# In the second half of a leg's rows, the up-rows are fetched up to twenty ahead of the down-rows

## The chip, the cores and the metric

The kernel runs on one core of one Trainium2 chip. The metric is the device time of one execution in microseconds. PE is TensorE, DVE is VectorE, ACT is ScalarE, POOL is GpSimd, SP is SyncE.

## The reference

Two layers of a hybrid encoder over 512 positions of 1024 features. Each layer adds a mix of three head groups to x, and then a retrieval from a table of 16384 experts (PEER). The part that sets this kernel's time is the retrieval, cut to its core:

```python
s1, s2 = scores of a query against 128 sub-keys each
v1, i1 = lax.top_k(s1, 16); v2, i2 = lax.top_k(s2, 16)
cand = v1[..., :, None] + v2[..., None, :]
top_s, pos = lax.top_k(cand, 16)            # per head, 8 heads
experts = take_along_axis(i1*128 + i2, pos) # 8 x 16 = 128 experts per position
gates = softmax(top_s)
act = gelu(einsum('tkd,td->tk', peer_u[e], h))
out = einsum('tk,tkd->td', gates * act, peer_v[e])
```

So each position needs 128 rows of `peer_u` and 128 rows of `peer_v`, each 1024 float32.

## The kernel before

The 512 positions are 4 tiles of 128, one position in each partition, and there are two layers, so 8 tiles pass. The program runs in ten legs, n = 0 to 9, one behind the other, with a meeting of all engines between two. Leg n computes the mixers and the routing (the choice of experts) of tile n, and beside them the retrieval of tile n-1. "First" tiles of a layer (legs 0 and 4) have more to do and tables of their own. Leg 8 has no mixers left, and leg 9 ends the last tile. Below, "leg 2" is n = 2. Leg 1 starts at 251.83 us of the span.

**Up-rows** are fetches of `peer_u`: k-th expert of all 128 positions, 128 rows of 4 KB, into one of 8 buffers `ringU` (`fetch_u`, L226). VectorE multiplies each with h and sums it: a **dot** (`gathered`, L803; semaphore `dots`). A leg takes 128 of them; the first eight go by `idx_w` at the end of the leg before, the others by `idx_g`. The first fetch by `idx_w` is used here as the mark of a leg's start. **Down-rows** are fetches of `peer_v` into 8 buffers `ringV` (`fetch_v`, L236). TensorE mixes them in groups of four rows with the weights `wm` (`mix`, L479; semaphore `mixed`); a group is 16 matmuls in the trace and 8 with two column halves in the order's rows. A leg fetches 128 down-rows: 56 for the second half of tile n-2's experts (its first eight were fetched at the end of the leg before), then 64 for the first half of tile n-1's, then eight ahead for the next leg. Leg 1 has no tile n-2 and leaves out the 56. Numbered 1 to 128 in GpSimd's order, down-row j belongs to ring row j+7.

All fetches are issued by GpSimd, in one queue and in program order. Its loop goes in steps of four rows, r0 = 8, 12, ... 124: four up-rows, then four down-rows. It waits before each: up-row k (from 1) for `dots` of k-8 at least, down-row j for `mixed` of j at least. Only the first comes before the second in the queue, so a wait for a dot also holds back the down-rows behind it, and the other way round.

The engines' other work is laid between by tables of counts: `DOTS` says how many dots VectorE has done by each stage (`heads`, `values`, `x1`, `queries`, `routing`), `MIX` how many groups TensorE has mixed by then. `queries` is the point just ahead of the routing. The routing on VectorE starts with sixteen MAX8 over the key scores (L1207, waits for TensorE's L733), then FIND_INDEX8 and MATCH_REPLACE8 (L1210, L1211), MAX8 and FIND_INDEX8 again (L1216, L1219), the candidates (L1226 to L1239), their second eight (L1243, L1246), the gates (L1253) and the expert numbers (L1286 to L1299). It has seven gaps in which dots are done, the seven numbers of `routing`: behind eight and sixteen fields, behind L1219, behind L1239, behind L1246, and two in the expert numbers.

Weights of 2 MB a piece come by SP's queue: w_in, w_out and peer_w_q, into two buffers `wring`.

## Time and profile before

| | us |
|---|---|
| median of 3 runs | 3650.46 (3648.02 to 3655.35) |
| the profiled execution | 3636.02 |
| its span, first to last instruction | 3634.2 |
| VectorE busy | 2227.8 (61%) |
| GpSimd busy | 2283.0 (63%) |
| TensorE busy | 1836.1 (51%) |
| DMA, mean over the span | 353 GB/s |

Durations are read from one profiled execution and set against its own time. In the timelines below a row starts with its start and its duration in us; the bracket at its end has the idle time of the engine just before it and what ended that. "issue" there means that the profile shows nothing that was waited for.

### The profile page before, as it was taken

Reading aid. Unit: us, or ns where it says so; the run is one execution under the profiler, and the core shown is the slowest. Engines: PE = TensorE matmul, PEld = TensorE weight load, DVE = VectorE, ACT = ScalarE, POOL = GpSimd, SP = SyncE. Lnnn points to the kernel's source line nnn. Section 1 sums busy time; section 2 is a strip of 40 time slices with the busy share of each in tenths; the row PEclk is TensorE's granted clock in tenths of the full one; section 3 lists DMA queues with packets and bytes.
Section 4 is the critical chain, followed back from the end, with each engine's and each line's share of the span. In section 5 each row is a group of like instructions: output and inputs, shape, how many; then the busy total and the mean of one; then the engine's idle time right before and its main releaser. Section 6 shows DMA issues by size and latency. Waiting matters only on the chain.

```text
span 3634.2 us, 30323 instructions
## 1 busy us (share of the span) xinstructions
PE 1836.1 (51%) x10176; PEld 894.3 (25%) x10176; DVE 2227.8 (61%) x5807; ACT 250.6 (7%) x683; POOL 2283.0 (63%) x2067
## 2 busy tenths in 40 slices
PE   6825452736454562566636455465636465233333
PEld 4425230513132230231304122232304122000000
DVE  6267757675768557765486746676585856645420
ACT  1200100001000100101000010001000110000000
POOL 0015667677667667555666766777676776767653
PEclk9767575767677776776758677676857676555666
DMA  6547899999999999999999999999999999999996
GB/s 247 211 158 267 302 409 342 357 369 390 379 352 368 337 406 364 407 415 405 382 375 374 349 360 396 343 378 361 398 370 366 358 370 412 361 362 378 361 344 232
DMA packets 314671, 1282.62 MB, mean 353 GB/s; under 512 B 34955, under 2 KB 35211, under 8 KB 303507
## 3 DMA queue, kind: packets, MB, share of 16 engines
q0 software_dynamic: 294912, 1073.87, 78.2%
q1 hardware_dynamic: 18740, 201.83, 13.7%
q10 hardware_dynamic: 864, 4.99, 0.4%
q8 instruction: 82, 1.34, 0.1%
q14 instruction: 73, 0.59, 0.0%
HBM read 1272.16 MB, written 8.39 MB: 352 GB/s over the span
## 4 chain that ended last, share of the span: by engine, by line
POOL 31%; PE 18%; DVE 16%; DMA 16%; issue 14%; another core or an unknown queue 5%; ACT 1%; SPq 0%; POOLq 0%; DVEq 0%; ACTq 0%
POOL ringV L236 18%; POOL ringU L226 13%; DMA ringV<-in_peer_v,idxP 9%; PE py L479 6%; DVE ringU L803 5%; DMA ringU<-in_peer_u,idx_g 5%; PE pj L551 4%; DMA ringU<-in_peer_u,idx_w 2%; PE pj L718 1%; PE pj L622 1%; PE pj L494 1%; PE pj L558 1%; PE pw L692 1%; PE pw L519 1%
## 5 line engine op out<-in xcount | busy, mean ns | idle before, releaser
L803 DVE CUSTOM_DVE_ANT_0 ringU<-ringU,h2g 128x1024 f32<-128x1024 f32 x1024 | 1224.6, 1225 | 800.0 <-DMA ringU<-in_peer_u,idx_g 549.7
L236 POOL DMA_INDIRECT ringV<-in_peer_v,idxP x1024 | 1144.6, 1118 | 581.4 <-issue 272.3
L479 PE MATMUL py<-ringV,wm 128*32 128x512 f32 x4096 | 817.8, 914 | 1125.2 <-DMA ringV<-in_peer_v,idxP 924.8
L226 POOL DMA_INDIRECT ringU<-in_peer_u,idx_g x960 | 1071.4, 1116 | 472.1 <-issue 284.2
L479 PEld LDWEIGHTS py<-ringV,wm 128*32 128x32 f32 x4096 | 160.3, 145 | 1646.9 <-issue 1575.9
L551 PE MATMUL pj<-hT,wring 128*128 128x128 f32 (+1 forms) x2560 | 329.8, 292 | 26.7 <-issue 18.8
L551 PEld LDWEIGHTS pj<-hT,wring 128*128 128x128 f32 (+1 forms) x2560 | 317.4, 201 | 63.3 <-issue 50.7
L226 POOL DMA_INDIRECT ringU<-in_peer_u,idx_w x64 | 62.2, 971 | 269.4 <-DVE gate_w L1299 246.1
L692 PE MATMUL pw<-hT,ckv_all 128*128 128x128 f32 x320 | 78.9, 401 | 94.1 <-issue 60.7
L718 PE MATMUL pj<-wring,mixT 128*128 128x512 f32 x256 | 118.3, 622 | 9.1 <-issue 8.4
L494 PE MATMUL pj<-ident,wk 128*128 128x128 f32 x168 | 43.5, 364 | 138.6 <-DVE wk L1165 61.3
L519 PE MATMUL pw<-wring,crep 128*32 128x512 f32 x384 | 67.1, 811 | 73.2 <-DVE crep L886 29.6
L829 DVE TENSOR_TENSOR py<-py,g2g 128x1024 f32<-128x1024 f32 x8 | 9.8, 1231 | 142.8 <-PE py L479 130.6
L494 PE MATMUL pj<-ident,hh 128*128 128x128 f32 x128 | 30.9, 422 | 119.4 <-DVE hh L1033 115.9
L678 PE MATMUL pw<-ckvT_all,hh 128*128 128x128 f32 (+3 forms) x128 | 65.7, 618 | 50.3 <-DVE cols L1171 40.1
L692 PEld LDWEIGHTS pw<-hT,ckv_all 128*128 128x128 f32 x320 | 61.8, 278 | 114.4 <-issue 67.6
L803 DVE DVE_READ_ACCUMULATOR2_ANT acts<- 128x1 f32 x1024 | 82.7, 81 | 0.0
L622 PE MATMUL pj<-wk,par 128*32 128x128 f32 x384 | 50.1, 356 | 49.1 <-DVE state L1084 38.6
L718 PEld LDWEIGHTS pj<-wring,mixT 128*128 128x128 f32 x256 | 50.6, 201 | 81.3 <-issue 80.2
L318 ACT ACTIVATE hT<-pj 128x512 f32<-128x512 f32 (+3 forms) x96 | 47.0, 489 | 336.5 <-PE pj L494 195.9
L494 PEld LDWEIGHTS pj<-ident,wk 128*128 128x128 f32 x168 | 25.3, 178 | 178.9 <-issue 97.0
L408 ACT ACTIVATE wk<-wk,cols 128x128 f32<-128x128 f32 (+3 forms) x64 | 35.8, 560 | 470.2 <-DVE cols L1171 291.9
(294 smaller groups left out, 1893.0 us busy)
## 6 DMA issues: line engine op xcount, KB each, us to landing
wring<-in_w_in SPq DMA_DIRECT2D x28, 2048.0 KB
wring<-in_w_mod SPq DMA_DIRECT2D x24, 2048.0 KB
wring<-in_w_out SPq DMA_DIRECT2D x16, 2048.0 KB
wring<-in_peer_w_q SPq DMA_DIRECT2D x16, 2048.0 KB
ringV<-in_peer_v,idxP POOLq DMA_INDIRECT x1024
ringU<-in_peer_u,idx_g POOLq DMA_INDIRECT x960
wring<-in_w_in SPq DMA_DIRECT2D x8, 784.0 KB
x_mix<-xs SPq DMA_DIRECT2D x8, 512.0 KB
```

The lines of the kernel that those rows point to most:

```text
L226: pool.indirect_dma_start(out=ringU[k % NR][:, :], out_offset=None, in_=ux, in_offset=bass.IndirectOffsetOnAxis(ap=idx[:, k:k + 1], axis=0 ...
L236: pool.indirect_dma_start(out=ringV[r % NR][:, :], out_offset=None, in_=vx, in_offset=bass.IndirectOffsetOnAxis(ap=idx[:, at:at + 1], axis=0),
L318: a.activation(dst, src, ACT.Copy).then_inc(S[sem], 1)
L479: mm = t.matmul(py[32 * j:32 * j + 32, c * 512:(c + 1) * 512], wm[e % 2][:, at:at + 32], ringV[(4 * m + j) % NR][:, c * 512:(c + 1) * 512] ...
L494: m = t.transpose(dst, src, ident[:, :])
L519: mm = t.matmul(pw[32 * j:32 * j + 32, at:at + 512], crep[:, k * 32:(k + 1) * 32], wt[:, k * 512:(k + 1) * 512], start=k < 4, stop=k >= 4)
L551: mm = t.matmul(dst, wt[:, k * gc + c0:k * gc + c0 + width], hT[:, k * 128:(k + 1) * 128], start=k == 0, stop=k == KT - 1)
L622: mm = t.matmul(dst, C[:, cs], wk[:, at + m * 128:at + (m + 1) * 128], start=i == 0, stop=i == 3)
L678: t.matmul(pw[:, (h % 2) * 512:(h % 2) * 512 + W], q, ckvT_all[:, 0:W], start=True, stop=True).then_inc(S["lg_ps"], 1)
L692: mm = t.matmul(pw[:, 1024 + (h % 4) * 128:1152 + (h % 4) * 128], ckv_all[:, s * 128:(s + 1) * 128], hT[:, (h % 2) * 512 + s * 128:(h % 2) ...
L718: mm = t.matmul(pj[n][:, :], mixT[:, k * 128:(k + 1) * 128], wt[:, k * 512:(k + 1) * 512], start=k == 0, stop=k == KT - 1)
L803: v.tensor_tensor_reduce(out=ringU[k % NR][:, :], in0=ringU[k % NR][:, :], in1=h2g[:, :], scale=1.0, scalar=0.0, op0=ALU.mult, op1=ALU.add ...
```

## The change

In the legs whose tile is not the first of a layer and that have mixers (1, 2, 3, 5, 6, 7), GpSimd's loop fetches, from r0 = 64 on, up-rows further than the step's own four: `ups_by` gives the number of groups of four that are fetched by step i = r0/4. It is i+1 as before below 16, and i+1+(i-15)//2 from there, 128 rows at most. So steps 17, 19, 21, 23 and 25 have eight up-rows, and 128 are reached in step 26. `DOTS` lets VectorE do more of them ahead of the routing (106 where there were 95), and `MIX` has one or two groups fewer by each stage from the last head on (21 where there were 23 ahead of the key scores; the semaphores' limits are unchanged). `MIX_FIRST` is written without `MIX` as its base and keeps its numbers.

```diff
@@ -58,15 +58,15 @@
-        "picked": [38 + (r + 1) * 10 // 16 for r in range(16)], "heads": [48 + (h + 1) * 26 // 8 for h in range(8)],
-        "values": 82, "x1": 83, "queries": 95, "routing": [101, 107, 113, 117, 120, 122, 124]}
+        "picked": [38 + (r + 1) * 10 // 16 for r in range(16)], "heads": [48 + (h + 1) * 28 // 8 for h in range(8)],
+        "values": 86, "x1": 89, "queries": 106, "routing": [110, 113, 116, 119, 121, 123, 125]}
...
-       "heads": [12, 13, 14, 15, 16, 16, 16, 18], "values": 19, "x1": 20, "h2": 21, "queries": [22, 23], "routing": 28}
+       "heads": [12, 13, 14, 15, 16, 16, 16, 17], "values": 18, "x1": 19, "h2": 20, "queries": [21, 21], "routing": 27}
@@ -80,6 +80,11 @@
+def ups_by(b, i):
+    n = i + 1 if b is None or is_first(b) or 4 * i < HE else i + 1 + (i - 15) // 2
+    return min(n, T // 4)
@@ -238,11 +243,13 @@
+                up = NR
                 for r0 in range(NR, T, 4):
                     if u is not None:
-                        for r in range(r0, r0 + 4):
+                        for r in range(up, 4 * ups_by(b, r0 // 4)):
                             pool.wait_ge(S["dots"], r - NR + 1)
                             fetch_u(r, idx_g)
+                        up = 4 * ups_by(b, r0 // 4)
```

GpSimd at the end of leg 2, from step 26 (before), to the first fetches for the next leg (x4 means four fetches):

```order
L226 DMA ringU<-in_peer_u,idx_g 128x1024 x4
L236 DMA ringV<-in_peer_v,idxP 128x1024 x4
L226 DMA ringU<-in_peer_u,idx_g 128x1024 x4
L236 DMA ringV<-in_peer_v,idxP 128x1024 x4
L226 DMA ringU<-in_peer_u,idx_g 128x1024 x4
L236 DMA ringV<-in_peer_v,idxP 128x1024 x12
L226 DMA ringU<-in_peer_u,idx_w 128x1024 x8
```

The same queue after, from step 23:

```order
L231 DMA ringU<-in_peer_u,idx_g 128x1024 x8
L241 DMA ringV<-in_peer_v,idxP 128x1024 x4
L231 DMA ringU<-in_peer_u,idx_g 128x1024 x4
L241 DMA ringV<-in_peer_v,idxP 128x1024 x4
L231 DMA ringU<-in_peer_u,idx_g 128x1024 x8
L241 DMA ringV<-in_peer_v,idxP 128x1024 x4
L231 DMA ringU<-in_peer_u,idx_g 128x1024 x4
L241 DMA ringV<-in_peer_v,idxP 128x1024 x32
L231 DMA ringU<-in_peer_u,idx_w 128x1024 x8
```

Down-rows 97 to 128 now stand behind the last up-row in one piece of 32, where the longest was 12. All line numbers behind the tables are higher by five to seven.

TensorE in leg 2 before, from the projection of the outputs (L718) to the end of the mixing; L733 are the key scores, L551 the queries:

```order
L718 MATMUL pj<-wring,mixT 128x512 x16
L479 MATMUL py<-ringV,wm 32x512 x8
L494 MATMUL pj<-ident,hh 128x128 x8
L479 MATMUL py<-ringV,wm 32x512 x8
L551 MATMUL pj<-hT,wring 128x128 x32
L479 MATMUL py<-ringV,wm 32x512 x8
L551 MATMUL pj<-hT,wring 128x128 x32
L479 MATMUL py<-ringV,wm 32x512 x8
L733 MATMUL pw<-par,pr 128x128 x16
L479 MATMUL py<-ringV,wm 32x512 x72
```

And after (L725, L558 and L740 are those three):

```order
L725 MATMUL pj<-wring,mixT 128x512 x16
L486 MATMUL py<-ringV,wm 32x512 x8
L501 MATMUL pj<-ident,hh 128x128 x8
L486 MATMUL py<-ringV,wm 32x512 x8
L558 MATMUL pj<-hT,wring 128x128 x32
L486 MATMUL py<-ringV,wm 32x512 x8
L558 MATMUL pj<-hT,wring 128x128 x32
L740 MATMUL pw<-par,pr 128x128 x16
L486 MATMUL py<-ringV,wm 32x512 x88
```

Two groups of down-rows moved behind the key scores: eleven groups stand there instead of nine.

## Rows read from the trace of the kernel before

**Rows 1.** The page, part 3: GpSimd's DMA queue, packets, MB, share of 16 engines.

```profile
q0 software_dynamic: 294912, 1073.87, 78.2%
```

**Rows 2.** Busy time by stretch, leg 2 (stretch, us, each engine's, PEclk, DMA share, GB/s).

```profile
869.30:937.00 67.70, 39.87 (x253) 26.39 (x251) 33.69 (x98) 4.45 (x10) 39.51 (x38) 0.74 1.02 411
969.30:1027.90 58.60, 19.44 (x92) 4.56 (x92) 47.91 (x142) 0.84 (x3) 45.11 (x37) 0.61 0.92 326
```

**Rows 3.** Timeline of POOL: the starts of legs 2, 3, 5, 6, 7, 8.

```profile
619.27 0.94 POOL L226 DMA_INDIRECT ringU<-in_peer_u,idx_w  x1 [0.30 <-issue]
1027.98 0.94 POOL L226 DMA_INDIRECT ringU<-in_peer_u,idx_w  x1 [0.30 <-issue]
1910.17 0.93 POOL L226 DMA_INDIRECT ringU<-in_peer_u,idx_w  x1 [4.39 <-DVE acts L803]
2321.67 0.94 POOL L226 DMA_INDIRECT ringU<-in_peer_u,idx_w  x1 [0.30 <-issue]
2731.02 0.93 POOL L226 DMA_INDIRECT ringU<-in_peer_u,idx_w  x1 [0.30 <-issue]
3139.77 0.94 POOL L226 DMA_INDIRECT ringU<-in_peer_u,idx_w  x1 [0.30 <-issue]
```

**Rows 4.** Timeline of DVE: the routing's first MAX8, legs 2, 5, 7.

```profile
925.22 0.89 DVE L1207 MAX8 pr<-pw 128x8 f32<-128x128 f32 x4 [6.80 <-PE pw L733]
2213.16 2.08 DVE L1207 MAX8 pr<-pw 128x8 f32<-128x128 f32 x10 [1.44 <-PE pw L733]
3036.12 2.08 DVE L1207 MAX8 pr<-pw 128x8 f32<-128x128 f32 x10 [2.12 <-PE pw L733]
```

**Rows 5.** Timeline of PE: second group behind the key scores, legs 2, 5, 7.

```profile
938.76 1.94 PE L479 MATMUL py<-ringV,wm 128*32 128x512 f32 x8 [8.42 <-DMA ringV<-in_peer_v,idxP]
2232.05 2.79 PE L479 MATMUL py<-ringV,wm 128*32 128x512 f32 x12 [6.58 <-DMA ringV<-in_peer_v,idxP]
3054.35 1.94 PE L479 MATMUL py<-ringV,wm 128*32 128x512 f32 x8 [6.58 <-DMA ringV<-in_peer_v,idxP]
```

**Rows 6.** Timeline of DVE: starts and ends of the routing's pieces, leg 2.

```profile
932.77 1.21 DVE L803 CUSTOM_DVE_ANT_0 ringU<-ringU,h2g 128x1024 f32<-128x1024 f32 x1
...
941.07 0.09 DVE L1210 MATCH_VALUE_LOAD pr<-pr,pw 128x8 f32 x1
...
945.32 1.22 DVE L803 CUSTOM_DVE_ANT_0 ringU<-ringU,h2g 128x1024 f32<-128x1024 f32 x1
...
953.82 3.19 DVE L1216 MAX8 pr<-wk 128x8 f32<-128x128 f32 x16
...
962.12 0.29 DVE L1219 FIND_INDEX8 pr<-pr,wk 128x8 uint32<-128x128 f32 x1 [1.07 <-issue]
...
973.99 0.68 DVE L1226 TENSOR_TENSOR wk<-pr 128x512 f32<-128x512 f32 x1
...
980.75 1.23 DVE L803 CUSTOM_DVE_ANT_0 ringU<-ringU,h2g 128x1024 f32<-128x1024 f32 x1
...
985.34 1.50 DVE L1243 MAX8 pr<-wk 128x8 f32<-128x112 f32 x8
...
988.96 1.22 DVE L803 CUSTOM_DVE_ANT_0 ringU<-ringU,h2g 128x1024 f32<-128x1024 f32 x1
...
990.11 1.22 DVE L803 CUSTOM_DVE_ANT_0 ringU<-ringU,h2g 128x1024 f32<-128x1024 f32 x1
```

**Rows 7.** Timeline of POOL: two waits among the last tile's down-rows.

```profile
3533.63 0.94 POOL L236 DMA_INDIRECT ringV<-in_peer_v,idxP  x1 [3.84 <-PE py L479]
...
3547.22 0.94 POOL L236 DMA_INDIRECT ringV<-in_peer_v,idxP  x1 [3.97 <-PE py L479]
```

**Rows 8.** Timeline of POOL: the fetch of down-row 65 in leg 3.

```profile
1260.35 0.93 POOL L236 DMA_INDIRECT ringV<-in_peer_v,idxP  x1 [6.57 <-PE py L479]
```

**Rows 9.** Busy time by stretch, leg 3, columns as in Rows 2.

```profile
1248.00:1268.00 20.00, 14.49 (x86) 8.05 (x84) 11.22 (x24) 4.28 (x11) 10.68 (x11) 0.69 0.69 236
```

**Rows 10.** Timeline of POOL: a fetch beside dots in the routing, leg 2.

```profile
970.59 1.99 POOL L236 DMA_INDIRECT ringV<-in_peer_v,idxP  x1 [0.30 <-issue]
```

More of the change, by code:

```diff
@@ L67 @@
 MIX = {"start": 1, "projected": [2, 3, 4, 5], "states": 6, "gated": 7, "picked": 11,
-       "heads": [12, 13, 14, 15, 16, 16, 16, 18], "values": 19, "x1": 20, "h2": 21, "queries": [22, 23], "routing": 28}
-MIX_FIRST = dict(MIX, mod=[0, 1, 1, 2, 9, 10, 11, 11, 12, 13, 14, 14], start=3, projected=[4, 6, 7, 8], states=10, gated=12,
+       "heads": [12, 13, 14, 15, 16, 16, 16, 17], "values": 18, "x1": 19, "h2": 20, "queries": [21, 21], "routing": 27}
+MIX_FIRST = dict(mod=[0, 1, 1, 2, 9, 10, 11, 11, 12, 13, 14, 14], start=3, projected=[4, 6, 7, 8], states=10, gated=12,
                  picked=15, heads=[15, 16, 16, 16, 18, 19, 19, 20], values=21, x1=22, h2=23, queries=[24, 25], routing=29)
```

## The prediction, made before the changed kernel was run

> **What bounds the kernel now.** I read the page's DMA queues first. GpSimd's queue moves 1073.87 MB and its packets fill 78.2% of 16 engines' span [rows 1]. The code makes 256 row fetches for each of 8 tiles, 2048 in all, so one fetch is 0.524 MB. The reader should see a kernel whose time is nearly that of its gathers. Everything else matters only where it delays one.
>
> Second, the table by stretch for leg 2 [rows 2]. From 869 to 937 us DMA moves 411 GB/s, one fetch per 0.524/0.411 = 1.28 us. In the last 59 us before the next leg only 326 GB/s move, while VectorE is busy 47.9 of 58.6 us. That is the routing stretch which the change thins out.
>
> Third, the marks of a leg. A leg starts with the first fetch by idx_w [rows 3]: leg 2 lasts 1027.98-619.27 = 408.7 us, leg 5 411.5, leg 7 408.8. Routing starts at the first MAX8 on the key scores [rows 4]: 305.9, 303.0 and 305.1 us into the leg. I call this point S. VectorE had waited there for TensorE's key scores (6.8, 1.4, 2.1 us), not for up-rows: its 95 dots were done. From S to the leg's end it takes 102.8, 108.5 and 103.7 us.
>
> So two things decide: when S comes, and how long the rest takes from S. The changed legs are 1, 2, 3, 5, 6 and 7. Legs 4 and 8 keep their order.
>
> **First part: S comes later.** I count the fetches of a leg in GpSimd's order, 1 to 256 (leg 1 lacks 56 down-rows, equally before and after). Before, dot 95 needs fetch 179: up-row 95 stands behind 84 down-rows. After, the table wants 106 dots before routing, and up-row 106 stands behind 84 down-rows: fetch 190. Running ahead does not hide this: the same bytes must land, in order, and from 869 to 937 us the queue has no hole in which eleven more could have come.
>
> When fetch 190 lands can be read. Down-rows 89 to 92 are fetches 189 to 192 before. TensorE mixes them as the second group behind the key scores and waits for exactly that landing [rows 5]: 938.76, 2232.05, 3054.35 us, or 319.5, 321.9, 323.3 us into legs 2, 5, 7. Fetch 190 is two earlier, 2.6 us; the dot on it takes about 1.2. So S would be 318.1, 320.5, 321.9: later by 12.2, 17.5 and 16.9 us. The other edits ahead of S (two dots more for the heads, four for values, six for x1) I cost at nothing. Their up-rows have the same fetch numbers as before or up to six more, and the wait for fetch 190 covers them; without that cover it would be six fetches, 7.7 us.
>
> **Second part: from S to the leg's end.** Moving 11 dots out takes 11 x 1.15 = 12.6 us of VectorE's time from routing. But GpSimd has one queue, and up-row k may be fetched only when dot k-8 is done. Down-row 97 now stands behind up-row 128, so behind dot 120. Dot 120 comes in the fifth gap of routing. With the durations of leg 2 [rows 6]: S to the first gap 932.77-925.22 = 7.55; then dots 107-110, 4.6 (a dot follows the last after 990.11-988.96 = 1.15); 945.32-941.07 = 4.25, three dots 3.45; 962.41-953.82 = 8.6 (end of the last FIND_INDEX8), three dots 3.45; 980.75-973.99 = 6.76, three dots 3.45; 988.96-985.34 = 3.62, dot 120, 1.15. Sum 46.9. Up-row 128 is then fetched, and down-row 97 starts at S+48.2.
>
> Behind it stand 32 down-row fetches in a row, where before the longest such run was 12. Only 8 buffers hold them, each free only when TensorE has mixed it. Leg 8's end shows such a run [rows 7]: GpSimd waits for TensorE at 3533.63 and again at 3547.22, eight fetches per 13.59 us. So down-row 121 starts three such rounds behind 97, 40.8 us, and its eight take 8 x 1.24 = 9.9, since a fetch that waits for nothing takes 0.94 and follows 0.30 behind the last [rows 3]. The leg ends at S+48.2+50.7 = S+98.9.
>
> That is shorter than now by 3.9, 9.6 and 4.8 us in legs 2, 5, 7. With the later S the legs become longer by 8.3, 7.9 and 12.1: mean 9.4, times six legs 56.6 us.
>
> **Third part: what the run-ahead fills.** In leg 3, GpSimd waits 6.57 us for TensorE before down-row 65, and DMA falls to 236 GB/s over 20 us [rows 8, 9], 3.5 MB or 8.5 us below the rate of 411. After, four more up-rows (77 to 80) are queued ahead of that wait; more can't be, since every later block of down-rows waits at the same fetch number. That returns at most 4 x 1.28 = 5.1 us a leg where the hole is deep, and nothing where there is none. Leg 3's hole is the only one shown, and I take 3 us as the mean of legs with deep and with shallow ones: 18 us for six. The bounds are 0 and 31.
>
> **The port.** Beside back-to-back dots a fetch takes 1.99 us of GpSimd instead of 0.94 [rows 10]. The cost of the dots that remain in routing lies between 0 (GpSimd waits there anyway) and two fetches per leg, 2.1 us. I take 0. The Trainium skill's page SBUF — State Buffer, section "SBUF: two separate sides", says that VectorE with two SBUF inputs and GpSimd share a port pair under an exclusive lock. The doubled fetch agrees with it. By that rule alone taking dots away from a stretch that GpSimd's issuing bounds would be a gain; it is the rival "faster" below. The skill's page DMA: Bandwidth & Descriptors, section "Anatomy of one DMA — SWDGE (gpsimd) path", gives 2.0 us plus bytes/436e3, which would be 3.2 us a fetch and would make the run of 32 faster than I have it; the 13.59 us round speaks against relying on it.
>
> **Sum.** 56.6-18 = +38.6 us on the profiled execution, 3636.0 us (span 3634.2 and 1.8 around it): 3674.6. The median of the runs shown, 3650.5, lies 14.4 above that execution, so 3689.
>
> **Rivals.** *Faster: routing is relieved and S stays.* If eleven more up-rows land by the time the key scores are there, each leg ends at the old S+98.9: -3.9, -9.6, -4.8, mean 6.1, six legs -37, so 3614. If filled holes come on top, less by up to 18: 3596. For it: VectorE is the busiest engine in the last 59 us, and DMA there has room (326 of 411 GB/s). Against: fetch 190 landed 11 to 16 us after S in the three legs [rows 4, 5]. It decides from a gain of about 9 to 13 fetches ahead of S, where at most 4 are in sight. Chance 0.22.
> *Nothing moves.* The holes give the whole 5.1 us, and the run of down-rows goes at 12 us a round, three rounds 4.8 us a leg, 29 for six: 56.6-31-29 is about zero, 3650. For it: groups of down-rows that follow a pause find TensorE idle. Chance 0.12. The change not doing what it says comes out here too: "up to twenty ahead" exists in the order alone, since the ring holds eight; were the landing order hardly altered, nothing would move.
> *Much slower: GpSimd's one queue waits twice.* If TensorE's groups behind the key scores also starve while up-rows 113 to 128 wait for dots, the ring is empty when the run of 32 begins, and one more round of 13.6 us a leg is lost: +38.6+82, 3771. Against: groups of down-rows 89 to 96 stand between. Chance 0.06.
>
> **How the numbers follow.** Forecast 0.60, with its own range from its bounds: holes at 5.1 us and no port cost, 56.6-31 = +26 (3676), to no holes and the port's 12.6, +69 (3720). The range of 0.8 must reach into the faster rival to leave no more than 2 in 10 out: 3614 to 3720. About 0.2%, 7 us, is what a measurement of this kernel can tell from no change. Faster 0.23, same 0.12, slower 0.65.
>
> **What would show it.** Right: MAX8 on the key scores starts 315 to 322 us into legs 2, 5, 7 after a wait for an up-row's DMA; GpSimd waits for dots before up-rows 115, 122, 125 and 128; the last 32 down-rows take rounds near 13.6 us with TensorE as releaser; the leg is 412 to 421 us; dot 128 is done well ahead of the leg's end. Wrong: S at 306 with no wait for DMA, which gives the faster rival; or rounds of 12 us and less; or DMA above 400 GB/s until the last down-rows. If up-row 106 has another fetch number than 190, the first part falls.

## The result, and the profile of the changed kernel

The changed kernel takes 3708.23 us (median of 4 runs, 3703.64 to 3710.77). The kernel before, run beside it, takes 3649.24 us (4 runs, 3643.87 to 3655.35). The ratio is 1.0155 with the interval [1.0127, 1.0183]: slower by 59 us, where the forecast was slower by 38.6. The profiled executions lie further apart, 3710.77 against 3636.02 us, or 74.8.

The page of the changed kernel: part 3, GpSimd's DMA queue, and of part 4 the chain by engine. The bytes are those of [rows 1] and spread over a longer span, so the share falls from 78.2% to 77.5%.

```profile
q0 software_dynamic: 294912, 1073.87, 77.5%
...
POOL 29%; DVE 21%; DMA 17%; PE 16%; issue 12%; another core or an unknown queue 4%; ACT 0%; SPq 0%; POOLq 0%; DVEq 0%; ACTq 0%
```

The marks of a leg come first, as in [rows 3]: the timeline of POOL with the first fetch by idx_w of legs 2, 3, 5, 6, 7 and 8 (start, duration, instruction, idle time before it and what ended it).

```profile
629.17 0.94 POOL L231 DMA_INDIRECT ringU<-in_peer_u,idx_w  x1 [0.30 <-issue]
...
1052.24 0.94 POOL L231 DMA_INDIRECT ringU<-in_peer_u,idx_w  x1 [0.30 <-issue]
...
1940.45 1.19 POOL L231 DMA_INDIRECT ringU<-in_peer_u,idx_w  x1 [0.30 <-issue]
...
2361.43 0.94 POOL L231 DMA_INDIRECT ringU<-in_peer_u,idx_w  x1 [0.30 <-issue]
...
2787.13 0.94 POOL L231 DMA_INDIRECT ringU<-in_peer_u,idx_w  x1 [0.30 <-issue]
...
3216.35 0.94 POOL L231 DMA_INDIRECT ringU<-in_peer_u,idx_w  x1 [0.30 <-issue]
```

S, the first MAX8 of routing, is read as in [rows 4], in the timeline of DVE, legs 2, 5 and 7:

```profile
950.93 2.27 DVE L1214 MAX8 pr<-pw 128x8 f32<-128x128 f32 x11 [4.99 <-PE pw L740]
...
2260.24 2.86 DVE L1214 MAX8 pr<-pw 128x8 f32<-128x128 f32 x14
...
3113.66 2.47 DVE L1214 MAX8 pr<-pw 128x8 f32<-128x128 f32 x12
```

Leg 2 lasts 1052.24-629.17 = 423.1 us, of which 950.93-629.17 = 321.8 lie ahead of S. All legs, both kernels, read in the same way:

| leg | length before | after | S before | after | S to the end, before | after |
|---|---|---|---|---|---|---|
| 1 | 367.4 | 375.8 | 260.7 | 274.9 | 106.7 | 100.9 |
| 2 | 408.7 | 423.1 | 305.9 | 321.8 | 102.8 | 101.3 |
| 3 | 413.4 | 423.6 | 311.5 | 322.1 | 101.9 | 101.5 |
| 5 | 411.5 | 421.0 | 303.0 | 319.8 | 108.5 | 101.2 |
| 6 | 409.3 | 425.7 | 303.7 | 325.6 | 105.6 | 100.1 |
| 7 | 408.8 | 429.2 | 305.1 | 326.5 | 103.7 | 102.7 |

Leg 4, whose order is unchanged, goes from 468.8 to 464.7 us. The six changed legs give +79.3 us: S comes later by 100.8 us in all, and what follows S is shorter by 21.5. With leg 4 that makes +75.2 us, and the profiled executions lie 74.8 apart. Counted by S, the loss lies ahead of S, and what follows pays back about a fifth of it. This split should not be read as the place of the loss: S marks another point of the queue in each kernel, fetch 179 before and fetch 190 after. Fetch by fetch it looks different, as the run of the kernel before again shows below.

What follows S is seen in leg 7. The timeline of POOL, from up-row 115 to down-row 121 (L231 fetches up-rows, L241 down-rows):

```profile
3122.71 1.68 POOL L231 DMA_INDIRECT ringU<-in_peer_u,idx_g  x1 [6.91 <-DVE acts L810]
...
3142.51 1.68 POOL L231 DMA_INDIRECT ringU<-in_peer_u,idx_g  x1 [3.16 <-DVE acts L810]
...
3159.83 1.68 POOL L231 DMA_INDIRECT ringU<-in_peer_u,idx_g  x1 [2.91 <-DVE acts L810]
3161.82 0.94 POOL L241 DMA_INDIRECT ringV<-in_peer_v,idxP  x1 [0.30 <-issue]
...
3176.16 1.75 POOL L241 DMA_INDIRECT ringV<-in_peer_v,idxP  x1 [2.43 <-PE py L486]
...
3190.68 0.94 POOL L241 DMA_INDIRECT ringV<-in_peer_v,idxP  x1 [2.21 <-PE py L486]
...
3203.13 0.94 POOL L241 DMA_INDIRECT ringV<-in_peer_v,idxP  x1 [0.84 <-PE py L486]
```

The first three rows are up-rows 115, 122 and 128, each waiting for a dot. Directly behind up-row 128 stands down-row 97, at 3161.82-3113.66 = S+48.2. The last three are down-rows 105, 113 and 121: rounds of 14.3, 14.5 and 12.5 us per eight, with TensorE's mixing as releaser, and 13.2 us more to the leg's end. Dots are no longer what ends a leg: in leg 7 dot 128 is done at 3182.5, 34 us ahead of the end. Before, down-row 97 was fetched 22 to 24 us behind S, and 79 to 85 us followed it.

Busy time by stretch (stretch, its us, busy time and instructions of PE, PEld, DVE, ACT and POOL, then PEclk, DMA share, GB/s), ahead of S in leg 2 and for the run of last down-rows in leg 7:

```profile
881.00:949.00 68.00, 33.90 (x209) 23.90 (x202) 32.36 (x60) 4.00 (x8) 40.13 (x39) 0.69 1.02 412
...
3165.00:3216.00 51.00, 20.12 (x108) 4.48 (x108) 19.30 (x41) 1.45 (x6) 32.38 (x30) 0.67 0.88 302
```

The first answers to the 411 GB/s of [rows 2]. The second is the new tail: VectorE is busy only 19.3 of 51 us, where before it was busy 47.9 of 58.6 ([rows 2], leg 2), yet DMA moves 302 GB/s instead of 326. VectorE was relieved there and the transfers became no faster.

### The profile page after: what moved, and what is told of

Its sections match the earlier page's. It is cut to its first block, busy times and chain, and to the rows that moved or that the text cites. A ratio compares the mean times of both kernels' runs of the same rounds, so it can differ in the third digit from the quotient of the medians.

```text
span 3709.0 us, 30323 instructions
## 1 busy us (share of the span) xinstructions
PE 1867.9 (50%) x10176; PEld 911.5 (25%) x10176; DVE 2224.7 (60%) x5807; ACT 252.2 (7%) x683; POOL 2298.9 (62%) x2067
## 3 DMA queue, kind: packets, MB, share of 16 engines
q0 software_dynamic: 294912, 1073.87, 77.5%
q10 hardware_dynamic: 864, 4.99, 0.3%
## 4 chain that ended last, share of the span: by engine, by line
POOL 29%; DVE 21%; DMA 17%; PE 16%; issue 12%; another core or an unknown queue 4%; ACT 0%; SPq 0%; POOLq 0%; DVEq 0%; ACTq 0%
POOL ringV L241 16%; POOL ringU L231 13%; DVE ringU L810 8%; DMA ringV<-in_peer_v,idxP 7%; DMA ringU<-in_peer_u,idx_g 7%; PE py L486 6%; PE pj L558 4%; DMA ringU<-in_peer_u,idx_w 2%; PE pj L629 1%; PE pj L725 1%; DVE pr L1217 1%; DVE wk L1218 1%; DVE pr L1226 1%; PE pj L501 1%
## 5 line engine op out<-in xcount | busy, mean ns | idle before, releaser
L241 POOL DMA_INDIRECT ringV<-in_peer_v,idxP x1024 | 1132.2, 1106 | 608.2 <-PE py L486 279.0
L231 POOL DMA_INDIRECT ringU<-in_peer_u,idx_g x960 | 1097.2, 1143 | 508.5 <-issue 278.1
L486 PE MATMUL py<-ringV,wm 128*32 128x512 f32 x4096 | 832.4, 916 | 1087.5 <-DMA ringV<-in_peer_v,idxP 860.7
L558 PE MATMUL pj<-hT,wring 128*128 128x128 f32 (+1 forms) x2560 | 328.5, 292 | 20.5 <-issue 11.5
L558 PEld LDWEIGHTS pj<-hT,wring 128*128 128x128 f32 (+1 forms) x2560 | 316.4, 202 | 56.1 <-issue 43.6
L231 POOL DMA_INDIRECT ringU<-in_peer_u,idx_w x64 | 64.7, 1010 | 266.9 <-DVE gate_w L1306 247.7
L725 PE MATMUL pj<-wring,mixT 128*128 128x512 f32 x256 | 117.4, 618 | 10.7 <-issue 8.5
L501 PEld LDWEIGHTS pj<-ident,hh 128*128 128x128 f32 x128 | 25.1, 223 | 189.2 <-DVE hh L1040 162.1
L725 PEld LDWEIGHTS pj<-wring,mixT 128*128 128x128 f32 x256 | 50.2, 199 | 78.7 <-issue 75.2
```

The source lines that it names most:

```text
L231: pool.indirect_dma_start(out=ringU[k % NR][:, :], out_offset=None, in_=ux, in_offset=bass.IndirectOffsetOnAxis(ap=idx[:, k:k + 1], axis=0 ...
L241: pool.indirect_dma_start(out=ringV[r % NR][:, :], out_offset=None, in_=vx, in_offset=bass.IndirectOffsetOnAxis(ap=idx[:, at:at + 1], axis=0),
L486: mm = t.matmul(py[32 * j:32 * j + 32, c * 512:(c + 1) * 512], wm[e % 2][:, at:at + 32], ringV[(4 * m + j) % NR][:, c * 512:(c + 1) * 512] ...
L501: m = t.transpose(dst, src, ident[:, :])
L558: mm = t.matmul(dst, wt[:, k * gc + c0:k * gc + c0 + width], hT[:, k * 128:(k + 1) * 128], start=k == 0, stop=k == KT - 1)
L725: mm = t.matmul(pj[n][:, :], mixT[:, k * 128:(k + 1) * 128], wt[:, k * 512:(k + 1) * 512], start=k == 0, stop=k == KT - 1)
```

## The experiments

Theory: GpSimd has one queue in order. Down-rows stand behind up-rows whose dots the routing does late, so a leg ends when up-row 128 is fetched, plus a run of 32 down-rows through 8 buffers; and S moves with up-row 106's place in the queue. Rivals: the late S alone is the loss; the dots for x1 hold up the mixers; TensorE's mixing sets the run's pace.

The kernel before took about 3570 us beside the kernels that follow, not 3649. So each kernel is set against the runs of before that were made beside it, by ratio; a difference in us between two kernels that were not run side by side is rough.

**The changed kernel again.** No edit: a base for the rest.

> The changed kernel itself, beside the others of this call, because the kernel before took 3570 us beside the last four runs where it had taken 3649: times of different calls can't be set against one another, their ratios can. First measurement: 1.0155. On the faster memory of the last call, S came at 318 to 320 us; theory (one queue) says S+48.2 for down-row 97 whatever the memory, and S+101 to 102 for the leg's end, so that the ratio is no lower there: 1.015 to 1.025.

3651.02 us, 1.0217 [1.02, 1.0234]. S stands at 315.3 to 321.9 us in legs 2, 3, 5, 6 and 7, and the leg ends at S+101 to S+102.8, with down-row 97 at S+48.1 or S+48.2 in every changed leg. More frequent here are GpSimd's waits for dots ahead of S. Its timeline in leg 7, 272.8, 275.4 and 308.0 us into the leg:

```profile
3036.51 0.94 POOL L231 DMA_INDIRECT ringU<-in_peer_u,idx_g  x1 [4.35 <-DVE acts L810]
3039.03 1.78 POOL L231 DMA_INDIRECT ringU<-in_peer_u,idx_g  x1 [1.58 <-DVE acts L810]
...
3071.70 1.81 POOL L231 DMA_INDIRECT ringU<-in_peer_u,idx_g  x1 [9.44 <-DVE acts L810]
```

These are up-rows 98, 99 and 109. Up-row 98 needs dot 90, and the stage x1 allows 89; dot 90 comes only behind the norm. Up-row 109 needs dot 101, and that dot waits for no stage but for its own row, in the timeline of DVE:

```profile
3070.20 1.22 DVE L810 CUSTOM_DVE_ANT_0 ringU<-ringU,h2g 128x1024 f32<-128x1024 f32 x1 [10.02 <-DMA ringU<-in_peer_u,idx_g]
```

Up-row 101 was fetched at 3047.52, 22.7 us earlier. So the longest of these waits is a wait for the transfers. In the first measurement's leg 3 the wait before up-row 98 is 4.98 us:

```profile
1333.24 1.68 POOL L231 DMA_INDIRECT ringU<-in_peer_u,idx_g  x1 [4.98 <-DVE acts L810]
```

**The kernel before again.**

> The kernel before, for a trace beside the last two calls' traces: ratio 1.000. With it e7's gain of 0.8% can be placed. Theory: in e7 no fetch of the last 54 waits for a dot of routing, so that from down-row 97 to the leg's end it takes 78.5 us (read in e7), 2 to 5 us less than in the kernel before, and the rest of the 5 us a leg comes from waits for dots ahead of down-row 97 that go away.

3558.02 us, where the runs of the same kernel beside it have 3570.53: 0.9973 [0.9949, 0.9996]. Two sets of runs of one kernel lie 0.3% apart, so a ratio within 0.3% of 1 proves nothing here. Against its legs, those of the changed kernel again have S later by 12.9 us on average and 0.6 us more behind S: 13.5 us a leg, six legs 81, near the 79 us between 3651.02 and the 3572.11 beside it. What follows S is no shorter here, so the 21.5 us that it gave back in the first measurement are not repeated.

The same fetch of GpSimd's queue can be set against itself. Its start, in us into the leg, mean of legs 2, 3, 5, 6 and 7 (read from the timelines of POOL):

| | fetch 190 | fetch 210 | fetch 250 | the leg's end |
|---|---|---|---|---|
| before | 303.2 | 336.6 | 399.1 | 410.3 |
| changed | 303.9 | 344.7 | 414.3 | 424.5 |
| before again | 301.2 | 335.3 | 394.3 | 406.1 |
| changed again | 296.9 | 339.1 | 409.4 | 420.0 |

Fetches 190 and 250 of leg 2, before again (the leg starts at 616.64) and then changed again (626.67):

```profile
920.87 0.94 POOL L236 DMA_INDIRECT ringV<-in_peer_v,idxP  x1 [0.30 <-issue]
...
1012.26 1.20 POOL L236 DMA_INDIRECT ringV<-in_peer_v,idxP  x1 [0.30 <-issue]
```

```profile
921.80 0.94 POOL L231 DMA_INDIRECT ringU<-in_peer_u,idx_g  x1 [0.30 <-issue]
...
1032.64 0.93 POOL L241 DMA_INDIRECT ringV<-in_peer_v,idxP  x1 [0.30 <-issue]
```

Up to fetch 190 the changed kernel has lost 0.7 us in the first pair and nothing in the second. It loses 14.5 and 19.4 us on the 60 fetches behind it, where GpSimd's waits for dots and for TensorE grow from 10.0 to 25.3 us a leg in the first pair and from 7.0 to 28.7 in the second (fetches 191 to 256, same five legs, each wait counted above its usual 0.30). The second pair also shows what became of the holes: GpSimd issues fetch 190 4.3 us earlier, and by the trace's records of landings, which are complete enough in the later traces only, it lands at 316.9 us instead of 316.5. It is 20.1 us under way instead of 15.3.

**The late start undone.** Only 95 dots are wanted before routing, in the new order of fetches.

```diff
-        "values": 86, "x1": 89, "queries": 106, "routing": [110, 113, 116, 119, 121, 123, 125]}
+        "values": 86, "x1": 89, "queries": 95, "routing": [101, 107, 113, 117, 120, 122, 124]}
```

> The changed kernel, but VectorE does 95 dots ahead of routing and 101, 107, 113, 117, 120, 122, 124 in its gaps, as before the change; the fetch order stays. Theory (one queue): S comes back to the key scores, some 5 us earlier (about 315), but dot 120 then comes 59.5 us behind S, down-row 97 at S+61, and the leg ends near 315+61+53 = 429: 3 to 8 us longer than in the changed kernel, 3735. Rival (late start): the later S is the loss, so an S 5 to 10 us earlier gives 30 to 60 us back: 3665.

3683.87 us, 1.0317 [1.0291, 1.0342]: slower than the changed kernel by a hundredth, some 35 us. S is back at 292 to 305 us in legs 2 to 7. Leg 2 of it, timeline of DVE, then of POOL in a fence of its own:

```profile
937.25 3.27 DVE L1214 MAX8 pr<-pw 128x8 f32<-128x128 f32 x16 [17.17 <-PE pw L740]
```

```profile
946.30 1.68 POOL L231 DMA_INDIRECT ringU<-in_peer_u,idx_g  x1 [19.20 <-DVE acts L810]
...
1009.86 1.99 POOL L241 DMA_INDIRECT ringV<-in_peer_v,idxP  x1 [0.30 <-issue]
```

VectorE sits idle for 17.17 us before S, since the table gives it no dots. Then GpSimd waits 19.20 us before up-row 104, whose dot 96 comes in routing's first gap. Down-row 97 follows at 1009.86, S+72.6, and the leg ends 52.7 us later. Expected was S+61: from up-row 104 on, 41 fetches go out without a wait and take 63.6 us, 1.55 each, and that issuing was not in the sum. An early S thus buys nothing in this order. The rival "the late S alone is the loss" falls.

**Routing's dots earlier.** The changed kernel with more dots in the first gaps.

```diff
-        "values": 86, "x1": 89, "queries": 106, "routing": [110, 113, 116, 119, 121, 123, 125]}
+        "values": 86, "x1": 89, "queries": 106, "routing": [114, 120, 122, 123, 124, 126, 127]}
```

> The changed kernel with one edit: the dots in the routing's gaps come earlier, the seven numbers are 114, 120, 122, 123, 124, 126, 127 instead of 110, 113, 116, 119, 121, 123, 125. Work, fetch order and the 106 dots ahead of routing stay. Theory (one queue): down-row 97 stands behind up-row 128 and so behind dot 120; that dot now comes in the second gap, about 28 us behind S instead of 44.7, so down-row 97 goes from S+48 to about S+37 and each changed leg loses 11 us, the kernel some 60: 3645. Rival (late start): what costs is that routing starts 14 to 22 us later, and the rest follows from VectorE's own work, which this doesn't alter: 3708, no change. Rival (run of 32): the run is held back by DMA or TensorE, not by when it starts: within 10 us of 3708.

3616.32 us, 1.0138 [1.0115, 1.0162]: 28 us below the changed kernel by the ratios and 35 by the times, 5 to 6 a leg, where 11 were expected. Dot 120 came at S+30.6, near the 28 that were forecast. Down-row 97 did not follow it closely. Timeline of POOL, leg 2 (S at 936.59):

```profile
945.64 1.68 POOL L231 DMA_INDIRECT ringU<-in_peer_u,idx_g  x1 [6.92 <-DVE acts L810]
...
976.99 0.94 POOL L231 DMA_INDIRECT ringU<-in_peer_u,idx_g  x1 [0.30 <-issue]
978.23 1.43 POOL L241 DMA_INDIRECT ringV<-in_peer_v,idxP  x1 [0.30 <-issue]
```

Up-row 115 waits for the first gap. From there to down-row 97 GpSimd issues 22 fetches without one wait over 0.3 us, and that takes 978.23-945.64 = 32.6 us, 1.48 each. So S+9.05+32.6 = S+41.6 is the least that this order allows at this rate of issuing, and the routing's later gaps add 6.6 to it in the changed kernel. The direction of the theory holds; the second floor, GpSimd's own issuing, was missed.

**Up-rows 125 to 128 later.** They are held back until 16 of the last 32 down-rows are fetched.

```diff
     n = i + 1 if b is None or is_first(b) or 4 * i < HE else i + 1 + (i - 15) // 2
+    if b is not None and not is_first(b) and i < T // 4 - 2:
+        n = min(n, T // 4 - 1)
     return min(n, T // 4)
```

> The changed kernel, but the last four up-rows (125 to 128) are fetched only in step 30, ahead of down-row 113, instead of in step 26; all else stays. Theory (one queue): down-row 97 no longer stands behind dots 117 to 120 but behind 116 only (about S+32), and follows down-rows 93 to 96 at about S+38 instead of S+48; four up-rows more in the run behind it cost nothing to 5 us. Legs 5 to 10 us shorter, 3708-45 = 3663. Rival (run of 32 itself is the loss, whenever it begins) also says shorter, but only by breaking the run: its rounds of eight down-rows would shrink from 14 to near 10 us around the four up-rows. Rival (late start): no change, 3708.

3631.38 us, 1.018 [1.0157, 1.0203]: 13 us less than the changed kernel by the ratios and 20 by the times, not 45, and the intervals touch. Timeline of POOL, leg 2, with down-rows 97, 105, up-row 125 and down-row 113:

```profile
979.70 1.97 POOL L243 DMA_INDIRECT ringV<-in_peer_v,idxP  x1 [0.30 <-issue]
...
994.62 0.94 POOL L243 DMA_INDIRECT ringV<-in_peer_v,idxP  x1 [0.30 <-issue]
...
1007.96 0.94 POOL L233 DMA_INDIRECT ringU<-in_peer_u,idx_g  x1 [0.30 <-issue]
...
1012.93 0.94 POOL L243 DMA_INDIRECT ringV<-in_peer_v,idxP  x1 [0.30 <-issue]
```

Down-row 97 comes at S+38.8 instead of S+48.1, 9.3 us earlier. But the round in which four up-rows now stand takes 1012.93-994.62 = 18.3 us. They were not free: from down-row 97 to the leg's end it takes 59.4 us instead of 53.1 in this leg, and 5.1 us more on the mean of six, the upper end of the 0 to 5 that I had allowed. Of the 9.3 us a leg, 4.2 are left.

**The x1 dots back.** The stages values and x1 ask for the old numbers.

```diff
-        "values": 86, "x1": 89, "queries": 106, "routing": [110, 113, 116, 119, 121, 123, 125]}
+        "values": 82, "x1": 83, "queries": 106, "routing": [110, 113, 116, 119, 121, 123, 125]}
```

> The changed kernel with 82 and 83 dots by the stages values and x1 instead of 86 and 89. The prediction costed these at nothing, under the cover of the wait for fetch 190. If the cover holds, S stays where fetch 190 lands, 320 to 326 us into a leg, and the time is within 7 us of 3708. Rival: they delay the norm ahead of the queries (it came 7 to 13 us later than before the change) and with it TensorE's key scores and two weight loads, and that is why S came 2 to 5 us later than forecast and no hole was filled: 5 us a leg back, 3678.

3653.1 us, 1.0236 [1.0215, 1.0257], not to be told from the changed kernel. The norm (its row L1040) starts at 249 to 264 us in legs 2 to 7, some 17 earlier than in the changed kernel again, and the key scores end at 289 to 297 instead of 296 to 305. S stays at 314 to 321.5. In leg 2 VectorE, with the key scores long there, waits for an up-row with S next (timeline of DVE):

```profile
943.19 1.23 DVE L810 CUSTOM_DVE_ANT_0 ringU<-ringU,h2g 128x1024 f32<-128x1024 f32 x1 [5.16 <-DMA ringU<-in_peer_u,idx_g]
...
945.63 2.47 DVE L1214 MAX8 pr<-pw 128x8 f32<-128x128 f32 x12
```

So what the six dots more for x1 cost is covered by the wait for the last up-rows, as the prediction said. The changed kernel again has that cover by itself: its key scores end 17 to 23 us ahead of S.

**Half of the mixing.** This kernel is the changed one and leaves out the first 512 of 1024 columns of the mixed rows, in all groups but the first and last of a tile. The fetches are the same.

```diff
-                        for c in range(2):
+                        for c in (range(2) if m in (HS, HS - 1) else (1,)):
```

> The changed kernel, which leaves out the first 512 columns of the mixing in all groups but the first and the last of a tile: half of TensorE's matmuls on down-rows, all fetches and waits as they are. It measures what of a round of eight down-rows in the run of 32 (13.5 to 15 us) is TensorE. If the round is issue, landing and mixing one behind the other, a group's 3.64 us at the lower clock becomes 1.82 and the round 12: five rounds' worth, 6 to 8 us a leg, 45 us in all against e6 (ratio near 1.009). If the landing alone sets it, less than 2 us a leg.

3614.61 us, 1.013 [1.0083, 1.0177]. Busy time by stretch, down-row 97 to the end of leg 2, here and then in the changed kernel again:

```profile
994.30:1044.50 50.20, 13.08 (x60) 2.53 (x60) 22.47 (x45) 0.53 (x2) 35.17 (x32) 0.50 0.92 320
```

```profile
989.90:1043.10 53.20, 21.73 (x108) 4.81 (x108) 22.80 (x45) 0.53 (x2) 33.98 (x32) 0.72 0.88 305
```

In leg 2 TensorE is busy 8.6 us less and the run shrinks by 3.0, from 53.2 to 50.2. Leg 2 is the smallest case: over the six legs the run goes from 53.9 to 49.5 us on average, 4.4 less, where 6 to 8 were expected, and TensorE's busy time in it from 22.2 to 13.1. So about half of the time taken from TensorE shows in the run. The granted clock differs, 0.50 here against 0.72 in leg 2 (0.55 to 0.72 in the other legs), so this is less than half the mixing at an equal clock would give. The rest of a round is issuing and the way of the rows: in the run a fetch lands a median 5.7 us after its start. As an estimate from these rows, three more fetches at 1.24, the 5.7 us and a group's mixing, 3.64 us where the granted clock is 0.50 (16 matmuls at 938.76 in the kernel before), make 13.1 us for a round of eight through two halves of the ring, one below the 14.0 that the rounds of the changed kernel again have on average. About 12 us more of the gain lie in legs 8 and 9.

**Only the thinner routing.** The kernel before with its own order of fetches; the tables of stages ahead of the queries are the old ones too.

```diff
-        "values": 82, "x1": 83, "queries": 95, "routing": [101, 107, 113, 117, 120, 122, 124]}
+        "values": 82, "x1": 83, "queries": 106, "routing": [110, 113, 116, 119, 121, 123, 125]}
```

> The kernel before with its own order of fetches, but 106 dots ahead of routing and 110, 113, 116, 119, 121, 123, 125 in its gaps: routing is thinned and nothing runs ahead. By the counting, up-row 106 is then fetch 202 and not 190, so S comes 12 fetches or 15 us later than in the changed kernel, about 330; the last 54 fetches follow with hardly a wait for a dot, at 1.35 to 1.5 us each: the leg ends at 410 to 415 us, or with routing's own end at S+74. 0 to 30 us more than before, ratio 1.000 to 1.010. Rival (late start is the loss): S is later than anywhere, so the ratio would be above 1.02.

3540.67 us, 0.9922 [0.9902, 0.9942]: 0.8% faster than the kernel before, where 0 to 30 us slower was expected. Beside the 0.3% between two sets of one kernel the gain is small but clear, and the six legs are 30 us shorter in the traces, though that of the kernel before again is of its slowest run. Leg 2, timelines of POOL and of DVE (a leg starts with L226 by idx_w, L236 is a down-row):

```profile
611.01 0.94 POOL L226 DMA_INDIRECT ringU<-in_peer_u,idx_w  x1 [0.30 <-issue]
...
934.92 1.79 POOL L236 DMA_INDIRECT ringV<-in_peer_v,idxP  x1 [0.76 <-issue]
...
1013.44 0.94 POOL L226 DMA_INDIRECT ringU<-in_peer_u,idx_w  x1 [1.16 <-DVE acts L803]
```

```profile
943.51 3.25 DVE L1207 MAX8 pr<-pw 128x8 f32<-128x128 f32 x16
...
1007.65 0.23 DVE L1294 CAST idx_w<-hT 128x128 uint32<-128x128 f32 x1
```

S stands at 943.51-611.01 = 332.5, later than in any other kernel, and the leg is 402.4 us long, against 416.5 for the changed kernel that was run beside it. Down-row 97 (934.92) is fetched 8.6 us ahead of S, no longer behind it. From it to the end it takes 78.5 us, much as in the kernel before (77.4). The next row, of the kernel before again, is its down-row 97 in leg 2, which starts at 616.64:

```profile
946.46 0.93 POOL L236 DMA_INDIRECT ringV<-in_peer_v,idxP  x1 [0.30 <-issue]
```

That is 329.8 us into the leg, against 323.9: the gain of the thinner routing is these 6 us, and 5.9 is also the mean of the six legs. In the kernel before again GpSimd waits 3.5 to 6.7 us for dot 96 (ahead of up-row 104), which comes in the first gap; here that dot is done ahead of S and the wait is gone. My expectation on the kernel before had put the gain behind row 97, and that was wrong.

A smaller step of the same kind, with 103 dots before routing:

```diff
-        "values": 82, "x1": 83, "queries": 95, "routing": [101, 107, 113, 117, 120, 122, 124]}
+        "values": 82, "x1": 83, "queries": 103, "routing": [108, 112, 115, 118, 120, 122, 124]}
```

> The kernel before with 103 dots ahead of routing and 108, 112, 115, 118, 120, 122, 124 in its gaps. In e7 (106) a leg ended 70.2 us behind S and 5 us behind the routing's last instruction, so VectorE's own work had become what ends the leg. Three dots fewer bring S forward by six fetches, 7.7 us, and lengthen the routing by 3.5: up to 4 us a leg less, unless the queue of fetches, some 3 us behind, takes over. 1 to 3 us a leg shorter than e7: ratio 0.987 to 0.991. If GpSimd waits for dots again: above 0.992.

3545.08 us, 0.9945 [0.9923, 0.9966], where 0.987 to 0.991 was expected. The interval overlaps with that of 106, and the second set of the kernel before lies within 0.3% of it, so its gain is not certain. S comes 7.2 us earlier on average than with 106, and from S to the end it takes 7.6 us longer. That fits a leg whose end is set by the queue of fetches and not by VectorE's own work, as I had it.

**Only the run-ahead, and less of it.** One group of four ahead from step 17 on, with the old tables.

```diff
-    n = i + 1 if b is None or is_first(b) or 4 * i < HE else i + 1 + (i - 15) // 2
+    n = i + 1 if b is None or is_first(b) or 4 * i < HE + 4 else i + 2
```

> All tables of the kernel before, and up-rows one group of four ahead from step 17 on, never more; the run of down-rows at the leg's end is 16 and not 32. S stays at the key scores. Theory (one queue): down-row 113 now needs dot 120 (S+66 to S+73 before the change too, when down-row 113 itself came at S+71), so nothing is held back for longer, and the wait for TensorE in the middle of the leg has four up-rows in front of it: 0 to 5 us a leg shorter than before, ratio 0.992 to 1.000. Rival (running ahead costs by itself, through the run of down-rows): four more in the run, 1.5 us a leg, 1.003.

3632.79 us, 1.0166 [1.0122, 1.021], where a gain or nothing was expected. One group ahead suffices for most of the loss: down-row 97 comes 7 to 24 us later into the leg than in the kernel before again. Timelines of POOL and DVE, leg 2:

```profile
934.38 1.67 POOL L231 DMA_INDIRECT ringU<-in_peer_u,idx_g  x1 [19.62 <-DVE acts L810]
```

```profile
925.34 3.26 DVE L1214 MAX8 pr<-pw 128x8 f32<-128x128 f32 x16 [22.55 <-PE pw L740]
...
932.89 1.21 DVE L810 CUSTOM_DVE_ANT_0 ringU<-ringU,h2g 128x1024 f32<-128x1024 f32 x1
```

Up-row 104 stands four fetches further forward and its dot 96 stands where it was, in the first gap at 932.89. So the whole gain in position is spent waiting, with the down-rows behind it: 16.1 to 23.4 us in the six legs, against 3.5 to 6.7 in the kernel before again. TensorE's key scores come 4 us sooner in this leg and up to 11 us later in the others.

The same order with the routing's dots moved forward:

```diff
-"routing": [101, 107, 113, 117, 120, 122, 124]}
+"routing": [103, 111, 117, 120, 122, 123, 125]}
```

> The last one, with the dots in the routing's gaps at 103, 111, 117, 120, 122, 123, 125 instead of 101, 107, 113, 117, 120, 122, 124. If waits for dots still hold back the queue in routing (before, GpSimd waited some 10 us a leg for dots there), they shrink by up to 4 us a leg: 0.985 to 0.997. If VectorE only waits longer for the same rows, the same as e8.

3628.28 us, 1.0149 [1.0129, 1.0168]: no difference that can be told. The wait before up-row 104 is 20.18 us there in leg 2. More dots in the gaps don't help, since the first of them comes no earlier.

**Ahead in the middle, back in line behind.** The run-ahead stops at step 22 and is used up by step 26; 102 dots before routing, all else as before.

```diff
-    n = i + 1 if b is None or is_first(b) or 4 * i < HE else i + 1 + (i - 15) // 2
+    n = i + 1 if b is None or is_first(b) or 4 * i < HE else max(min(i + 1 + (i - 15) // 2, 26), i + 1)
```

> Up-rows run ahead as in the change up to step 22 (104 up-rows), then none is fetched for three steps, and from step 26 on four up-rows and four down-rows alternate as before the change; 102 dots ahead of routing, 107, 112, 116, 119, 121, 123, 125 in its gaps. Up-row 102 is fetch 182, so S is at the key scores (near 303), and down-row 97 stands behind up-row 108 only, dot 100. Theory (one queue): no run of 32, no wait for a routing dot: the leg ends near 400, ratio 0.985 to 0.995. Rival (running ahead costs by itself, wherever it is): above 1.000, as with one group ahead (1.017).

3603.41 us, 1.0091 [1.0048, 1.0133], where 0.985 to 0.995 was expected. Row 97 and the end are as short behind S as hoped (S+13 to 18.6, and 89 to 95), and S is late, at 315 to 323 in legs 2 to 7, this time with the key scores and not an up-row as the last to come. Timeline of POOL, leg 2, up-rows 91 and 92:

```profile
889.46 0.94 POOL L231 DMA_INDIRECT ringU<-in_peer_u,idx_g  x1 [8.59 <-DVE acts L810]
895.40 1.68 POOL L231 DMA_INDIRECT ringU<-in_peer_u,idx_g  x1 [5.01 <-DVE acts L810]
```

Up-row 92 needs dot 84, and the stage x1 allows 83. The norm lies between. GpSimd stands still 13.6 us with down-rows queued behind it that TensorE mixes ahead of the key scores. That these 13.6 us are what makes the key scores late fits the order of the groups; it was not tried apart.

## Why the prediction was right where it was, and where not

**First part, S later.** Forecast for legs 2, 5 and 7: 318.1, 320.5, 321.9, later by 12.2, 17.5 and 16.9. Measured: 321.8, 319.8, 326.5, later by 15.9, 16.8 and 21.4. The reason holds: in legs 5 and 7 VectorE's last idle time before S was for an up-row's DMA. In the changed kernel again S is in all six legs the landing of fetch 190 and its dot (310.6 us on average, the landing 309.4), and with the key scores 4 to 10 us earlier (x1 dots back) S did not move. In the first measurement's leg 2 the key scores came last, by 4.99 us, with down-rows that had waited 13.16 us for TensorE behind them. Over the six legs S is later by 16.8 us on average instead of the 15.5 of the forecast; why by this little more is open.

**The edits costed at nothing.** Right for x1 and values, as the run with the old numbers shows; the two dots for the heads and the groups taken from `MIX` were not tried apart. One thing beside it was missed, that a table's number also holds a fetch: the 89 for x1 held up-row 98, 5 us in legs 3 and 5 of the first measurement and 4.1 to 5.0 us in all six legs of the second. With the old numbers that wait is gone and one before up-row 92 (1.8 to 5.0 us) stands in its place, with no change of the time that could be told. The prediction followed each stage's dots for VectorE, and not which fetch is next in GpSimd's queue when a stage holds its dots back.

**Second part, from S to the end.** Down-row 97 at S+48.2 was forecast and S+48.1 to 48.2 measured, in all six legs of each kernel with this order and this routing, in the first measurement as in the later, faster ones. GpSimd's waits before up-rows 115, 122 and 128 are there, but for the first two in leg 2, where the queue was late; that before 125 is hidden behind down-rows 93 to 96. The run of 32 was forecast at 50.7 us from leg 8's rounds of 13.59 [rows 7]; it measured 52.0 to 54.5, with rounds of 13.6 to 14.7, 13.9 to 15 and 12.4 to 13.8 us. From S to the end the legs became shorter by 3.6 us on average and not by 6.1: 2.5 us a leg, 15 in all.

**Third part, the filled holes: this step failed.** It took 18 us off, on the ground that four more up-rows queued ahead of a wait for TensorE would fill it. Up to fetch 190 the waits for TensorE did shrink, from 17.5 to 11.4 us a leg in the first pair and from 17.6 to 5.9 in the second (means of legs 2, 3, 5, 6 and 7), and those for dots grew, from 9.5 to 13.5 and from 12.1 to 17.9. In leg 3 the changed kernel has no wait left before down-row 65, where there were 6.57 us [rows 8]. In its place stand waits for dots, 7.9 us before up-row 74, 2.7 and 4.98 before 97 and 98, and the rate has a hole still, 215 GB/s where it was 236 in [rows 9] (leg 3, 210 to 230 us into it, columns as above):

```profile
1262.00:1282.00 20.00, 11.70 (x56) 7.48 (x52) 18.33 (x36) 5.95 (x16) 12.19 (x8) 0.75 0.65 215
```

The hole was moved from one ring to the other. And where GpSimd did come out ahead, by 4.3 us at fetch 190 in the second pair, the row landed no earlier. So the 3 us a leg were nothing at the point that decides S. The kernels with less run-ahead (one group, ahead and back) show the same at other places: 19.6 us before up-row 104, 8.6 and 5.0 before 91 and 92. A run-ahead by k rows asks for each dot k rows earlier, and VectorE's dots are bound to the stages of the mixers and to the landing of their own rows, 15 to 20 us behind the fetch there.

**The sum.** The six legs lost 79.3 us in the traces from which the forecast was built, 41 more than 38.6. Of these, 18 are the third part, 15 the longer stretch behind S, and 8 the later S (1.3 us a leg). By the medians the loss is 59 us; that this lies only 20 above the forecast is mostly due to the kernel before, whose profiled execution was 13 us faster than its median, and not to the reasoning. What the forecast had at the wrong place is the payback: in the second pair nothing behind S became shorter, and the loss of 81 us arises on fetches 191 to 256.

**The port at zero.** Right within what can be seen. Fetches beside dots take up to 1.99 us as in [rows 10]; in the changed kernel half of them take over 1.3 us and none does beside an idle VectorE. GpSimd's busy time is 2298.9 us instead of 2283.0, so taking eleven dots out of routing gave none of it back. The Trainium skill's page SBUF — State Buffer, section "SBUF: two separate sides", has a lock between the two engines whose holder blocks the other for a whole instruction. The long fetches agree with it; that as many fetches meet the dots in other stretches would explain the unchanged sum, and was not measured apart.

**The rivals.** "Faster: routing is relieved and S stays" needed nine to thirteen fetches ahead of S; none were gained, since fetch 190 landed as before. What it took for the kernel to be faster was the relief without the run-ahead (0.9922), with S at its latest: a start that is late costs nothing if GpSimd's queue keeps moving meanwhile. "GpSimd's one queue waits twice" did not occur in the changed kernel; the run with 95 dots, some 35 us slower, is near to it.

**What stays open.** Why the kernel before takes 3649 us in the first measurement and 3558 to 3572 in the later ones. Between the two traces of it, 27 of the 61 us lie in legs 8 and 9, and GpSimd's packets take 154 and 153 ns on average, so a faster memory is not shown. And how much of the late key scores in the ahead-and-back kernel comes from the waits at up-rows 91 and 92.

## What to carry to other kernels

Where one in-order queue feeds two rings, moving one stream's fetches forward gains only if their consumer also comes forward; check for every moved fetch what it waits for, and count what is queued behind it. The fetch that everything stands behind is found by counting in the queue. Its time was forecast to 0.1 us here, where the dots came last, and missed by 4.6 and 11.6 us in two experiments, where the issuing of the fetches between came last: both have to be summed. A hole in the transfer rate is not room until it is clear which of two waits would stand there next, and whether a row issued earlier also lands earlier. Compare two kernels at the same fetch, and not at a stage that has moved in the queue. When a change joins two ideas, try each alone: here one of them gained 0.8% and the other, with a smaller step, lost more than twice that.

## What the hardware showed that was not expected

- One and the same kernel took 3649.24 us in the first measurement and 3558.02 to 3572.11 in the later ones, 2.1 to 2.5% less, where the runs of one set lie within 1.1%. In the changed kernel down-row 97 stayed at S+48.1 to S+48.2 all the same.
- In the first two rounds of the run, eight fetches through eight buffers take 13.6 to 15 us. Taking 9.1 us of TensorE's busy time out of the run of 32 fetches shortened it by 4.4 (means of six legs, at a lower granted clock).
- From its start to its landing a fetch takes 6 to 8 us in most of a leg, and 15 to 20 us around fetch 190, where DMA moves 411 GB/s. There a fetch issued 4.3 us earlier landed at the same time.
- GpSimd issues fetches that wait for nothing at 1.24 us each beside an idle VectorE, and at 1.48 and 1.55 us on average over 22 and 41 of them in the routing.
